# Differential attention: the two score products of a head as a row-half pair, and the causal mask as a 16-bit matmul

## What is computed

```
s = einsum('pbhqd,pbhkd->bhqk' per part p, q_blk, k_blk)      # p = 0, 1; d = 64
mask = arange(nk)[None, :] <= (q_start + arange(nq))[:, None]
p = softmax(where(mask, s, neg), axis=-1)
w = p[0] - lam * p[1]
out = einsum('bhqk,bhkv->bhqv', w, v_blk)
```

## Time and profile before

| | |
|---|---|
| median of three runs | 3790.28 us |
| profiled execution | 3789.53 us, its span 3787.7 us |
| mean granted TensorE clock | 0.961 |
| PE busy | 3565.3 us (94% of the span) |
| DVE, ACT, POOL busy | 1827.5, 1178.8, 915.3 us |
| chain that ended last, by engine | PE 86%, issue 6%, DVE 3% |

### The profile page before, as it was taken

How to read it: one execution, slowest core, us unless ns; L and a number is a source line. 1 busy time by engine, 2 the same in 40 slices (tenths; PEclk the granted TensorE clock), 3 DMA queues, 4 the chain that set the end, 5 groups by cost and what they waited for, 6 DMA issues and landing times.

```text
span 3787.7 us, 45651 instructions
## 1 busy us (share of the span) xinstructions
PE 3565.3 (94%) x16352; PEld 2906.0 (77%) x16352; DVE 1827.5 (48%) x3647; ACT 1178.8 (31%) x1578; POOL 915.3 (24%) x371
## 2 busy tenths in 40 slices
PE   7999799999999998999999899989999989988998
PEld 6776578878888887888888688878887756666886
DVE  1354526974444535454554656454442343314573
ACT  3232334333444441121121332233332334423322
POOL 2301234442333334444454200000000421121000
PEclk8987899999999999999999899999999999989999
DMA  2200123444446455544545222222222211112222
GB/s 95 73 17 34 39 83 117 145 139 161 160 160 205 158 177 200 211 177 192 207 177 197 92 99 95 94 83 96 98 94 97 78 63 38 40 45 84 94 89 89
DMA packets 141175, 434.90 MB, mean 115 GB/s; under 512 B 11152, under 2 KB 44176, under 8 KB 132496
## 3 DMA queue, kind: packets, MB, share of 16 engines
q1 hardware_dynamic: 141072, 433.50, 32.8%
HBM read 364.25 MB, written 69.21 MB: 114 GB/s over the span
## 4 chain that ended last, share of the span: by engine, by line
PE 86%; issue 6%; DVE 3%; ACT 1%; DMA 1%; POOL 1%; SPq 0%; POOLq 0%; DVEq 0%; ACTq 0%
PE ring_banks L235 22%; PE ring_banks L237 22%; PE ring_banks L236 22%; PE work_banks L1064 3%; PE work_banks L237 3%; PE work_banks L235 3%; PE work_banks L236 3%; POOL wlo L709 1%; PE ring_banks L1225 1%; PE ring_banks L945 1%; PE work_banks L1194 1%; PE work_banks L1197 1%; PE work_banks L908 1%; DMA slot<-u 1%; PE work_banks L758 0%
## 5 line engine op out<-in xcount | busy, mean ns | idle before, releaser
L235 PE MATMUL ring_banks<-xx,wlo 128*128 128x512 f32 x2960 | 1178.1, 398 | 57.2 <-DVE xx L1674 39.7
L237 PE MATMUL ring_banks<-xx,whi 128*128 128x512 f32 x2960 | 1164.9, 394 | 0.0
L709 POOL TENSOR_TENSOR wlo<-slot,whi 128x1024 fp32r<-128x1024 f32 x235 | 578.9, 2467 | 2103.5 <-ACT whi L1277 2103.5
L236 PE MATMUL ring_banks<-xx,whi 128*128 128x512 f32 x2512 | 988.6, 394 | 0.0
L1277 ACT ACTIVATE whi<-slot 128x1024 fp32r<-128x1024 f32 x427 | 451.3, 1060 | 1073.9 <-DMA slot<-w 653.6
L235 PEld LDWEIGHTS ring_banks<-xx,wlo 128*128 128x128 f32 x2960 | 565.3, 191 | 183.1 <-issue 56.4
L237 PEld LDWEIGHTS ring_banks<-xx,whi 128*128 128x128 f32 x2960 | 563.6, 190 | 119.3
L236 PEld LDWEIGHTS ring_banks<-xx,whi 128*128 128x128 f32 x2512 | 479.1, 191 | 96.7
L722 POOL TENSOR_TENSOR vlo<-v,vhi 128x1024 fp32r<-128x1024 f32 x128 | 325.0, 2569 | 379.7 <-ACT vhi L1509 379.7
L1986 DVE TENSOR_SCALAR oneI<-const,slot_row,slot_gate 128x128 f32<-128x128 f32 x512 | 191.8, 375 | 289.7 <-PE work_banks L1064 275.9
L1641 DVE TENSOR_TENSOR wlo<-slot,whi 128x1024 fp32r<-128x1024 f32 x192 | 239.1, 1247 | 164.7 <-ACT whi L1277 153.6
(11 more groups left out here) (342 smaller groups left out, 4334.6 us busy)
## 6 DMA issues: line engine op xcount, KB each, us to landing
slot<-w SPq DMA_DIRECT2D x301, 512.0 KB, 3.3
slot<-u SPq DMA_DIRECT2D x128, 512.0 KB, 3.8
v<-v SPq DMA_DIRECT2D x32, 2048.0 KB, 11.6
early<-early SPq DMA_DIRECT2D x128, 256.0 KB, 3.9
gates<-stage SPq DMA_DIRECT2D x16, 2048.0 KB, 13.8
gbuf<-gates SPq DMA_DIRECT2D x32, 1024.0 KB, 4.8
ge<-early SPq DMA_DIRECT2D x32, 1024.0 KB, 7.3
hT<-xT SPq DMA_DIRECT2D x1, 2048.0 KB, 7.5
```

The costliest lines, as they stand in the source:

```text
L235: pe.matmul(out, w[1], x[0], start=start, stop=False)
L236: pe.matmul(out, w[0], x[1], start=False, stop=False)
L237: return pe.matmul(out, w[0], x[0], start=False, stop=stop)
L709: pool.tensor_tensor(w_lo, slot[s % RING], w_hi.bitcast(F32), ALU.subtract).then_inc(split, 1)
```

## The change

Within a score block the matmuls get another order, and the masks another type. For each cut of the keys, the score matmuls of part 0 (rows 0 to 63) and part 1 (rows 64 to 127) are issued directly behind one another, with `stop=False`. When all cuts are done, the masks follow, part 0 and part 1 of each cut, as matmuls of the bf16 identity with the bf16 mask table. The number of matmul calls stays: 4 for i < 3, and 8 for i = 3. A bf16 matmul leaves one record in the trace where the F32 one leaves two. Semaphores, waits and banks are as before.

```diff
-                for p in range(2):
-                    q = qT[64 * p:64 * p + 64, h, i * P:(i + 1) * P]
-                    at0 = 2 * T * p
-                    cuts = [0, keys] if i < TT - 1 else [0, T, keys]
-                    for k0, k1 in zip(cuts, cuts[1:]):
-                        c0 = max(k0, keys - P)
-                        mm = pe.matmul(psBf[:, at0 + k0:at0 + k1], q, kT[64 * p:64 * p + 64, h, k0:k1],
-                                       start=True, stop=c0 >= k1)
-                        if c0 < k1:
-                            mm = pe.matmul(psBf[:, at0 + c0:at0 + k1], ident, causal[:, c0 - keys + P:k1 - keys + P],
-                                           start=False, stop=True)
+                cuts = [0, keys] if i < TT - 1 else [0, T, keys]
+                for k0, k1 in zip(cuts, cuts[1:]):
+                    for p in range(2):
+                        q = qT[64 * p:64 * p + 64, h, i * P:(i + 1) * P]
+                        pe.matmul(psBf[:, 2 * T * p + k0:2 * T * p + k1], q, kT[64 * p:64 * p + 64, h, k0:k1],
+                                  start=True, stop=False)
+                for k0, k1 in zip(cuts, cuts[1:]):
+                    c0 = max(k0, keys - P)
+                    for p in range(2):
+                        mm = pe.matmul(psBf[:, 2 * T * p + c0:2 * T * p + k1], ident16, causal16[:, c0 - keys + P:k1 - keys + P],
+                                       start=False, stop=True)
                 mm.then_inc(a_s, 1)
```

## The result

The changed kernel took 3754.98 us (median of five runs, 3753.79 to 3758.68) against 3790.28 us before (3776.75 to 3790.76 over five runs). The ratio is 0.9918, with a 95% interval of 0.99 to 0.9935. The forecast was 3761; the time lies inside the stated range of 3744 to 3782, but outside the likeliest case's own range of 3757 to 3767, between that case and rival A. The profiled execution took 3755.19 us, with a span of 3753.4 us, so 34.3 us of span were gained. The profile before is from an execution of 3789.53 us, while others of that kernel took as little as 3776.75, so every gain that is read from that one profile may hold some microseconds that other executions of the kernel before do not lose.

What follows compares the result with a forecast made beforehand. TensorE's own time was taken as the bound nearly everywhere: 22.7 us from shorter score blocks plus 6 from the clock, 28.7 off 3789.5, gave 3761 us; stated range 3744 to 3782.

Steps and rivals of the forecast that it cites:

- likeliest case: Whole kernel: 22.7 us from shorter score blocks plus 6 from the clock, 3761 us (3757 to 3767); chance 0.43.
- rival A: All four slow-clock stretches behind the i = 3 blocks go: 38 us gained, 3751 us; chance 0.20.
- What bounds the stage: Differential attention, 170.8 to 400 us: TensorE (PE) is the bound nearly everywhere, busy 209.8 of 229.2 us.
- The cost of the new blocks: Sixteen score blocks: 0.58, 0.79, 1.00 and 1.53 us for i = 0 to 3, saving 25.4 us of TensorE time.
- rival B: Score pairs: the row halves do not overlap and only the masks gain, 10.4 us, 3779 us; chance 0.09.
- What reaches the end: Of the blocks' 25.4 us, 1.26 each lost at n = 5 and 9, and 0.2 at n = 4, leaving 22.7.
- the cap of 4.5 us: At n = 7, which has no filler, the vector engine's chain allows up to 4.5 us of gain.
- The clock: Slow stretches behind the four i = 3 blocks lose 18.1 us; at most 15.5 recoverable, 6 taken, the softest term.
- sister stage: The second network's latent attention (3125 to 3350 us), already using both new forms, with granted clock 0.98.
- C: The vector chain bounds all of n = 5 to 12: only 12.5 us gained, 3777 us; chance 0.10.
- D: PE idles longer at n = 5, 7, 9, 12 and the clock falls: 3778 or up to 3807 us; chance 0.13.
- E: The change does not do what it says, through queue order or bf16 mode switches: 3789 us; chance 0.05.

Runs made afterwards that it cites:

- e10: The new score block only at n = 5 and n = 9, against the kernel before: 3783.03 us, ratio 1.0.
- e7: The changed kernel run once more, on a second chip, against the kernel before: 3754.88 us, ratio 0.9907.
- e9: The whole change plus ten extra F32 dummy calls at the start, against the kernel before: 3743.69 us, ratio 0.9887.
- e8: The whole change with the score pairs of the i = 3 blocks computed three times, against the kernel before: 3753.96 us, ratio 0.9918.
- e1: The new order alone, masks still F32, against the kernel before: 3751.68 us, ratio 0.9905.
- e2: The bf16 masks alone, in the old order, against the kernel before: 3776.59 us, ratio 0.9977.
- e4: The whole change plus twenty extra F32 dummy calls at the start, against the kernel before: 3746.25 us, ratio 0.9894.
- e3: The whole change with both parts computed from rows 0 to 63, against the kernel before: 3768.16 us, ratio 0.9945.

## Why the prediction was right, and where it was not

*What bounds the stage.* Right. PE's own time decided, and e10 shows two places where it didn't; at n = 7 after the change it didn't either.

*The cost of the new blocks.* Right to 0.05 us for i = 1 and 2. The block with i = 3 was forecast 0.18 too long, because the 16-key pair and the short masks are cheap; that with i = 0 0.32 too short, because of the wait for ACT's copy, which the prediction didn't see. Over four heads 24.7 us at the full clock, against 25.4. One reading of the earlier trace rows mixes two measures: 1.09 us is the busy time of the old half with 512 keys, and from start to start it is 201.64 - 200.62 = 1.02. With that, rival B would be some 0.5 us faster than its 3779; nothing else hangs on it.

*What reaches the end.* The losses at n = 5 and 9 were 1.10 and 1.22 us, against 1.26 each, and no filler iteration had a new wait. At n = 7 there is a wait of 2.20 us; the prediction had let the full 2.57 of this block through, and laid the cap of 4.5 us on the clock's part. `turn` at n = 7 starts 17.4 us earlier than before and the one at n = 6 12.6 us (248.47 and 235.88), so this iteration gave 4.8 us: the cap was nearly right. If the wait of n = 7 is charged to the block, 24.7 - 1.1 - 1.2 - 2.2 = 20.2 us remain without the clock, where 22.7 were forecast.

*The clock.* This is the term that was mis-sized. "I take 6 of the 15.5" should have been all of it and more: the stage gained 45.5 us, so 25 of them came with the clock (the mean granted clocks, 40 us lost before and 11 now, give 29). In the profile of the change all four stretches behind the i = 3 blocks are at the full clock, as rival A had it, though not at n = 7 in e7 and e9; and a fifth at n = 10, which neither counted, went from 0.51 to 0.92 over 17 us (7 us). The evidence was in the earlier trace rows, the sister stage with the same forms and 0.98, and I gave it less weight than the waits between. e8 shows that the length of the block alone was not what counted. e1 and e2 show that the order was: with the F32 masks in the new order the clock stays, with bf16 masks in the old order it falls. That the changes of row count as such bring the low clock, rather than the pauses of the array around them or the one half of the rows at work in between, no run separates.

*What is missing.* The prediction had no term for code outside the stage: "the rest of the span as it was" is wrong by 11 us. The mask's type shortened the PE program by 40 matmul records and their loads, and that moved the one-hot loop to a place where each way back to its start costs a pause of 3.4 us, and one of the two a spell of low clock. Without it the kernel takes 3746 us (e4), 5 below rival A's 3751 and 15 below the forecast. The errors, 19 us too little from the clock against 2.5 too much from the blocks and 11 that came back, cancel for the most part: that the forecast is only 6 us off is luck.

*The rivals.* B falls by e3, C by the timeline (no wait at n = 6, 8, 10 or 11), D by the clock of 0.94, E by the blocks. A describes the stage. Two things stay open. The low stretch at n = 10 came and went between kernels with the old order in the block of n = 10 (0.51 and 0.60 in the two profiles of the old blocks, 0.86 in e10, 1.00 in e2), and the runs of the kernel before fall into two groups, near 3778 and near 3790; that one is the other's cause is argued, not shown. And why the place of a loop decides whether its code is brought again is not shown. The runs show the 17 packets, of some 16.5 kB each (0.28 MB in all), and which places did it.

## What to carry to other kernels

Where two matmuls of half the rows belong together, issue them directly behind one another, and put what needs all rows in front or behind: here that was worth more through the clock (some 25 us, in one pair of profiles) than through the overlap (9 us by the sum, 12.6 in e3). Price a change of order by what the clock does in the stretch behind it, and look for a stage of the same kernel that already has the new form; its granted clock is a row like any other. After any edit that changes the number of instructions, compare the untouched loops as well, by start times of the same instruction in both traces, and read the packets of the instruction queue; here ten dummy calls in an idle stretch gave back some 10 us.

## What the runs showed of the hardware

- The F32 score matmuls of both parts over 528 keys, 64 rows each, took 1.19 us together in different row halves, and 2.24 us in the same half.
- Blocks with four switches to 64 rows and back, one half of the rows at a time, were followed by a clock of 0.50 to 0.60 (before) and 0.57 to 0.79 (e2); blocks as long with one switch and both halves at once (e8) kept 1.00 in four of four.
- A wait of 4.78 us ahead of the level matmuls was followed by 16 records at the lower clock (3.78 us), and one of 2.20 us by 16 at the full one (2.02 us).
- The place of a loop's code cost 9 to 12 us in 564. It showed as a wait for "issue" at the loop's turns and as 17 or 18 more packets on the instruction queue, for shifts of -40 and +88 matmul records, and not for -20 to +24.
